# Dilated values of three head pairs made first with tokens on the partitions, and token factors spread by transposes

## The reference, cut to what matters

```
y = rms_norm(h) * g
qkv = (y @ w_qkv).reshape(B, S, 3, 3 groups, 8 heads, 64)        # 1024 x 4608 weights
for each group:  s = q k^T / 8 + bias over keys t - j*dilation;  m = max s;  p = exp(s - m)
                 den = sum p;  num = p v
o = (sum over groups of num * exp(m - m_all)) / (sum of den * exp(m - m_all))
h = h + o @ w_out
```

## Time and profile before

| | |
|---|---|
| median of 3 runs | 1863.96 us (1863.92 to 1864.14) |
| the profiled execution | 1863.83 us, span in the trace 1862.1 us |
| granted TensorE clock | 0.999 |
| TensorE busy | 1850.5 us, 99% of the span |
| TensorE weight loads busy | 1535.1 us, 82% |
| VectorE busy | 1127.5 us, 61% |
| ScalarE busy | 672.8 us, 36% |
| GpSimd busy | 165.3 us, 9% |
| chain that ended last | PE 94%, DVE 5% |

### The profile page before, as it was taken

The page is one execution under the profiler, slowest core; times in us unless marked ns, Lnnn a source line. Parts: engine busy times, 40 slices in busy tenths (PEclk is TensorE's granted clock), DMA queues, the critical chain, the costliest instruction groups (busy, mean ns, idle before and its releaser), DMA issues.

```text
span 1862.1 us, 24221 instructions
## 1 busy us (share of the span) xinstructions
PE 1850.5 (99%) x8817; PEld 1535.1 (82%) x8817; DVE 1127.5 (61%) x1524; ACT 672.8 (36%) x975; POOL 165.3 (9%) x199
## 2 busy tenths in 40 slices
PE   9999999999999999999999999999999999999998
PEld 7888888888888888888888888888888878888887
DVE  7888788676676444686642354366776786325532
ACT  6323434343333333344321222225555653212221
POOL 0011112200000011002000000101211220000000
PEclk9999999999999999999999999999999999999999
DMA  4222222323233333223333343322222123333232
GB/s 161 81 89 80 80 68 80 113 91 101 90 101 94 109 103 125 84 75 93 119 101 93 115 121 97 104 93 71 78 69 80 47 90 113 102 93 100 90 102 68
DMA packets 55156, 175.29 MB, mean 94 GB/s; under 512 B 6201, under 2 KB 12857, under 8 KB 55074
## 3 DMA queue, kind: packets, MB, share of 16 engines
q1 hardware_dynamic: 49744, 170.43, 29.4%
q10 hardware_dynamic: 4818, 3.68, 0.9%
q0 software_dynamic: 512, 0.03, 0.0%
HBM read 171.96 MB, written 2.13 MB: 93 GB/s over the span
## 4 chain that ended last, share of the span: by engine, by line
PE 94%; DVE 5%; DMA 0%; issue 0%; ACT 0%; SPq 0%; DVEq 0%; ACTq 0%
PE ps L605 30%; PE ps L607 29%; PE ps L606 29%; PE ps L1101 1%; DVE wlo L1621 1%; PE ps L1132 1%; PE ps L1113 1%; PE ps L613 1%; PE ps L903 1%; PE ps L893 0%; DVE yr L1640 0%; DVE grm L1713 0%; PE ps L1144 0%; PE ps L980 0%; DVE h L2286 0%
## 5 line engine op out<-in xcount | busy, mean ns | idle before, releaser
L605 PE MATMUL ps<-xhi,whi 128*128 128x512 f32 x1568 | 617.2, 394 | 1.4 <-DVE wlo L1621 0.6
L607 PE MATMUL ps<-xlo,whi 128*128 128x512 f32 x1568 | 610.9, 390 | 0.0
L606 PE MATMUL ps<-xhi,wlo 128*128 128x512 f32 x1568 | 610.5, 389 | 0.0
L1621 DVE TENSOR_TENSOR wlo<-raw,whi 128x1024 fp32r<-128x1024 f32 x314 | 403.8, 1287 | 210.8 <-ACT whi L1257 210.6
L1257 ACT ACTIVATE whi<-raw 128x1024 fp32r<-128x1024 f32 x314 | 331.1, 1055 | 537.6 <-PE ps L607 475.4
L605 PEld LDWEIGHTS ps<-xhi,whi 128*128 128x128 f32 x1568 | 294.4, 188 | 64.9 <-DVE wlo L1621 1.9
L607 PEld LDWEIGHTS ps<-xlo,whi 128*128 128x128 f32 x1568 | 294.3, 188 | 62.0
L606 PEld LDWEIGHTS ps<-xhi,wlo 128*128 128x128 f32 x1568 | 294.6, 188 | 59.3
L605 PE MATMUL ps<-mh,whi 128*128 128x512 f32 (+1 forms) x528 | 202.2, 383 | 0.0
L606 PE MATMUL ps<-mh,wlo 128*128 128x512 f32 (+1 forms) x528 | 202.0, 383 | 0.0
L607 PE MATMUL ps<-mh,whi 128*128 128x512 f32 (+1 forms) x528 | 202.0, 383 | 0.0
(11 more groups left out here) (346 smaller groups left out, 1962.4 us busy)
## 6 DMA issues: line engine op xcount, KB each, us to landing
raw<-wst SPq DMA_DIRECT2D x314, 512.0 KB, 3.5
h<-xT SPq DMA_DIRECT2D x8, 256.0 KB, 5.6
out<-h SPq DMA_DIRECT2D x8, 256.0 KB, 2.2
raw<-wst SPq DMA_DIRECT2D x4, 256.0 KB, 5.4
bias_a<-bias_rows ACTq DMA_DIRECT2D x4, 256.0 KB, 4.6
bias_b<-bias_rows ACTq DMA_DIRECT2D x4, 256.0 KB, 4.4
wsf<-wsT ACTq DMA_DIRECT2D x1, 512.0 KB, 3.4
bsb<-bs ACTq DMA_DIRECT2D x1, 512.0 KB, 4.3
```

Of the source, the lines that this page charges most:

```text
L605: pe.matmul(o, w[0], x[0], start=first, stop=False, **kw)
L606: pe.matmul(o, w[1], x[0], start=False, stop=False, **kw)
L607: return pe.matmul(o, w[0], x[1], start=False, stop=done, **kw)
L1621: dve.tensor_tensor(wlo[:, n % SLOTS, :], raw[:, n % 2, :], whi[:, n % SLOTS, :].bitcast(F32), ALU.subtract).then_inc(s_split, 1)
```

## The change

The 36 units of the dilated stage become 12 units `dv` and 27 units `dil`.

**`dv`: values of pairs 0 to 2 first.** For each group (f = 0 to 2 for groups 1, 2, 0 of the weights) four units hold rows of two k tiles each and 512 columns of V, of which the first 384 (pairs 0 to 2) are used. Now x is the stationary operand: 128 tokens (every fourth for f < 2) x 128 features, and 384 weight columns stream. Output: 128 tokens x 384 in each of four banks (`V_BANKS`). The norm stands behind the first of the 12 units. ScalarE reads the banks with the token's inverse rms as a scale (`v_kept_of`): pair 0 into `dvt`, pairs 1 and 2 kept in `vf` and `oM`; VectorE makes the low part of pair 0. The inverse rms with tokens on the partitions (`rtv`) comes over DRAM by three DMAs of GpSimd. GpSimd splits the kept values of pairs 1 and 2 into `dvt` between its steps (`kept_v_split`).

**`dil`: 27 units.** Pairs 0 to 2 have 6 units each (q and k), pair 3 has 9. All steps of pairs 0 to 2 come every 3 ticks. The last pair's v units are transposed as before (`v_turned`, 3 instead of 12), and both factor rows of pairs 0 to 2 go through bank 7, so that the second waits for the first's product (`s_fml`).

**Token factors** (lines 965 and 1055) are spread by `pe.transpose` where fp32 matmuls did it.

The diff, cut:

```diff
-          ("dil", 36), ("dilout", 4),
+          ("dv", 12), ("dil", 27), ("dilout", 4),
...
-DIL_UNITS = 36
+DIL_UNITS = 27
 LOGITS_AT, TURN_AT, SUMS_AT = {}, {}, {}
 V_TURN_AT, V_SPLIT_AT = {}, {}
 RESCALE_AT, WEIGHTS_AT, WIDEN_AT = {}, {}, {}
-for _p in range(4):
-    _d, _l = TICKS * (9 * _p + 6) - 1, TICKS * (9 * _p + 9)
-    for _s in range(4):
-        _n = 8 * _p + _s
-        LOGITS_AT[_d + 3 * _s], TURN_AT[_d + 3 * _s + 2], SUMS_AT[_d + 3 * _s + 5] = _n, _n, _n
-        _n += 4
-        if _p < 3:
-            _late = 1 if _s == 0 else 0
-            LOGITS_AT[_l + 5 * _s + 1 + _late], TURN_AT[_l + 5 * _s + 3 + _late] = _n, _n
-            SUMS_AT[_l + 5 * _s + (8 if _s < 3 else 7)] = _n
-        else:
-            LOGITS_AT[_l + (-2, -1, 1, 2)[_s]], TURN_AT[_l + (0, 1, 3, 4)[_s]], SUMS_AT[_l + 2 + _s] = _n, _n, _n
-    for _o in range(3):
-        _k = TICKS * (9 * _p + 3 * (_o + 1))
-        V_TURN_AT[_k + (1 if _k < TICKS * DIL_UNITS else 0)] = 3 * _p + _o
-        V_SPLIT_AT[_k + (2 if _k < TICKS * DIL_UNITS else 0)] = 3 * _p + _o
-    RESCALE_AT[_l + (18 if _p < 3 else 4)] = _p
-    WEIGHTS_AT[_l + (19 if _p < 3 else 5)] = _p
-    WIDEN_AT[_l + (20 if _p < 3 else 6)] = _p
+for _p in range(3):
+    for _s in range(8):
+        _n, _t = 8 * _p + _s, TICKS * (6 * _p + 4) + 3 + 3 * _s
+        LOGITS_AT[_t], TURN_AT[_t + 2], SUMS_AT[_t + 5] = _n, _n, _n
+    RESCALE_AT[_t + 2], WEIGHTS_AT[_t + 3], WIDEN_AT[_t + 4] = _p, _p, _p
+_l = TICKS * DIL_UNITS
+for _s in range(4):
+    _n, _t = 24 + _s, _l - 13 + 3 * _s
+    LOGITS_AT[_t], TURN_AT[_t + 2], SUMS_AT[_t + 5] = _n, _n, _n
+    _n += 4
+    LOGITS_AT[_l + (-2, -1, 1, 2)[_s]], TURN_AT[_l + (0, 1, 3, 4)[_s]], SUMS_AT[_l + 2 + _s] = _n, _n, _n
+RESCALE_AT[_l + 4], WEIGHTS_AT[_l + 5], WIDEN_AT[_l + 6] = 3, 3, 3
+for _o, _t in enumerate((_l - 23, _l - 10, _l)):
+    V_TURN_AT[_t], V_SPLIT_AT[_t + (1 if _o < 2 else 0)] = _o, _o
 PAIRED = STEPS - 4
 MULTIPLIED_AT = {}
 for _t, _n in LOGITS_AT.items():
     if _n >= PAIRED:
         MULTIPLIED_AT[_t] = (_n,)
     elif _n % 2 == 0:
-        MULTIPLIED_AT[_t - (3 if _n % 8 == 6 else 1)] = (_n, _n + 1)
+        MULTIPLIED_AT[_t - 1] = (_n, _n + 1)
 FACTOR_ROWS_AT = {}
 FACTORS_ON_AT = {}
 for _p in range(3):
     for _part in range(2):
-        FACTOR_ROWS_AT[TICKS * 9 * (_p + 1) + 22 + 3 * _part] = _p, _part
-        FACTORS_ON_AT[TICKS * 9 * (_p + 1) + 23 + 3 * _part] = _p, _part
-OUT_SPLIT_AT = {65: 0, 101: 1, 138: 2}
+        FACTOR_ROWS_AT[TICKS * 6 * _p + 46 + 2 * _part] = _p, _part
+        FACTORS_ON_AT[TICKS * 6 * _p + 47 + 2 * _part] = _p, _part
+OUT_SPLIT_AT = {53: 0, 77: 1, 102: 2}
 PART_AT = {TICKS * DIL_UNITS + _m: _m for _m in range(8)}
-OUT_HI_AT = {148: 0, 151: 1, 152: 2}
-OUT_LO_AT = {149: 0}
+OUT_HI_AT = {TICKS * DIL_UNITS + 4: 0, TICKS * DIL_UNITS + 7: 1, TICKS * DIL_UNITS + 8: 2}
+OUT_LO_AT = {TICKS * DIL_UNITS + 5: 0}
+V_BANKS = (2, 3, 4, 5), (0, 1, 6, 7), (2, 3, 4, 5)
...
         def factor_bank(p, part):
-            return bank(6) if part else bank(7 if p < 3 else 2)
+            return bank(7) if p < 3 else bank((2, 6)[part])
+        def v_tokens(f, t):
+            return slice(t, T, NT) if f < 2 else slice(t * P, (t + 1) * P)
+        def v_columns(f, t):
+            return rtv[:, (4 if f == 2 else 0) + t:(4 if f == 2 else 0) + t + 1]
+        def v_kept(p, o):
+            if o:
+                return vf[:, 1 + 2 * (o - 1):3 + 2 * (o - 1), :].rearrange("p a b -> p (a b)").rearrange(
+                    "p (t x c) -> p t x c", x=2, c=P)[:, :, p - 1, :]
+            return (oM[:, :] if p == 1 else vf[:, 0, :]).rearrange("p (t c) -> p t c", c=P)
+        def qkv_of(k):
+            return (k // 6, k % 6 // 2, k % 2) if k < 18 else (3, (k - 18) // 3, k % 3)
...
-                        ins = pe.matmul(bank(7 - n)[:, t * P:(t + 1) * P], rtk[:, NT * n + t:NT * n + t + 1].to_broadcast([P, P]), ident,
-                                        start=t == 0, stop=True, skip_group_check=True)
+                        ins = pe.transpose(bank(7 - n)[:, t * P:(t + 1) * P], rtk[:, NT * n + t:NT * n + t + 1].to_broadcast([P, P]), ident)
...
-                    ins = pe.matmul(bank(6)[:, t * P:(t + 1) * P], rtok[:, t:t + 1].to_broadcast([P, P]), ident, start=t == tiles[0],
-                                    stop=True, skip_group_check=True)
+                    ins = pe.transpose(bank(6)[:, t * P:(t + 1) * P], rtok[:, t:t + 1].to_broadcast([P, P]), ident)
...
                 if n % 4 == 0:
-                    pe.wait_ge(s_dvs, 3 * p + (3 if part else 2))
+                    if p == 0:
+                        pe.wait_ge(s_dve, 12 if part else 8)
+                    elif p < 3:
+                        pe.wait_ge(s_dvs, 3 * (p - 1) + (3 if part else 2))
+                    else:
+                        pe.wait_ge(s_dv3, 3 if part else 2)
                 if n:
                     pe.wait_ge(s_dco, n if n <= PAIRED else n - 1)
                 if n == STEPS - 1:
                     pe.wait_ge(s_dlg, STEPS)
-                if n % 8 == 0 and n:
-                    pe.wait_ge(s_fml, 2 * p)
...
             def v_turned(v):
-                pe.wait_ge(s_free, A0["dil"] + 3 * (v + 1))
+                pe.wait_ge(s_free, A0["dil"] + 18 + 3 * (v + 1))
                 if v:
-                    pe.wait_ge(s_dvs, v)
-                if v in (4, 7, 10):
-                    pe.wait_ge(s_fml, 2 * (v // 3) - 1)
+                    pe.wait_ge(s_dv3, v)
+                if v == 1:
+                    pe.wait_ge(s_fml, 6)
                 for t in range(NT):
-                    src = dvf[:, t * P:(t + 1) * P] if v % 3 == 2 else dvf[:, t::4]
+                    src = dvf[:, t * P:(t + 1) * P] if v == 2 else dvf[:, t::4]
                     ins = pe.transpose(bank(7)[:, t * P:(t + 1) * P], src, ident)
...
             def factor_rows(p, part):
                 pe.wait_ge(s_wid, 2 * p + part + 1)
-                if part or p == 3:
+                if p == 3:
                     pe.wait_ge(s_dco, 8 * p + 8)
-                else:
-                    pe.wait_ge(s_dvs, 3 * p + 4)
+                elif part:
+                    pe.wait_ge(s_fml, 2 * p + 1)
+                elif p == 2:
+                    pe.wait_ge(s_dv3, 1)
                 for t in range(NT):
...
-            for k in range(36):
-                xs = x_tile if k else fresh(x_tile, s_x, X0["down01"])
-                own = dict(banks=(DIL_BANK,) * 2, free=True) if k == 2 else {}
-                dense(U0["dil"] + k, A0["dil"] + k, full(1), xs, tick=lambda q: attend(TICKS * k + q), **own)
-                if k == 0:
-                    norm("down01")
-            for tick in range(TICKS * 36, LAST_TICK):
+            for f in range(3):
+                for j in range(4):
+                    u = U0["dv"] + 4 * f + j
+                    unit_ready(u)
+                    for k in (2 * j, 2 * j + 1):
+                        if f == 0:
+                            pe.wait_ge(s_x, X0["down01"] + k + 1)
+                        elif k == 0 and f == 1:
+                            pe.wait_ge(s_free, A0["dil"])
+                            pe.wait_ge(s_rb, N0["down01"] + 1)
+                        elif k == 0:
+                            pe.wait_ge(s_dve, 4)
+                        c0 = (k % 2) * T
+                        for t in range(NT):
+                            c = v_tokens(f, t)
+                            ins = mm3(pe, bank(V_BANKS[f][t])[:, 0:3 * P], (xhi[:, k, c], xlo[:, k, c]),
+                                      (whi[:, u % SLOTS, c0:c0 + 3 * P], wlo[:, u % SLOTS, c0:c0 + 3 * P]), k == 0, k == KD - 1)
+                    ins.then_inc(s_unit, 1)
+                    if f == 0 and j == 0:
+                        norm("down01")
+            pe.wait_ge(s_dve, 8)
+            for k in range(DIL_UNITS):
+                if k == 4:
+                    pe.wait_ge(s_dve, 12)
+                dense(U0["dil"] + k, A0["dil"] + k, full(1), x_tile, tick=lambda q: attend(TICKS * k + q))
+            for tick in range(TICKS * DIL_UNITS, LAST_TICK):
...
+            def v_kept_of(f):
+                if f != 1:
+                    act.wait_ge(s_rtw if f else s_rtv, 16)
+                act.wait_ge(s_unit, U0["dv"] + 4 * f + 4)
+                for t in range(NT):
+                    v, r = bank(V_BANKS[f][t]), v_columns(f, t)
+                    act.activation(dvt[:, f, t, 0::3, :], v[:, 0:P].rearrange("p (x d) -> p x d", d=DH), ACT.Copy, scale=r)
+                    if f == 0:
+                        act.activation(v_kept(1, 0)[:, t, :], v[:, P:2 * P], ACT.Copy, scale=r)
+                        ins = act.activation(v_kept(2, 0)[:, t, :], v[:, 2 * P:3 * P], ACT.Copy, scale=r)
+                    else:
+                        both = vf[:, 2 * f - 1 + t // 2, (t % 2) * 2 * P:(t % 2 + 1) * 2 * P]
+                        ins = act.activation(both, v[:, P:3 * P], ACT.Copy, scale=r)
+                    ins.then_inc(s_dvh, 1)
```

(81 more changed lines are left out.)

10 lines of the change are left out of this document (6 added, 4 removed).

## The result

The changed kernel takes 1873.59 us, median of five runs (1873.29 to 1873.84), against 1863.96 of the kernel before (five runs in turn with it): ratio 1.0049 with an interval of 1.0037 to 1.0060. It is 9.6 us slower, where 2.3 us faster was forecast; it lies above the range (1859.5 to 1867.0) and 1.0 above rival A's 1872.6. The spans of the two traces differ by 9.8 us.

A forecast was written before the change was run, and what follows sets the result against it. TensorE's queue was taken to set the end. The terms 0.94 - 3.8 + 1.2 - 0.9 - 0.4 + 0.7 gave -2.3 us, so 1861.7 us, 0.12% faster, with a range of 1859.5 to 1867.

The forecast's parts named there:

- rival A: First two V stages: strided weight loads are not hidden behind 384 columns, +10.9 us, giving 1872.6; chance 0.11.
- (1): V projections on TensorE: 288 matmuls of 384 columns replace 216 of 512, +0.94 us; strided loads charged nothing.
- The upper bound: V projections: a strided load takes twice about 0.115 us, 0.23, so 192 loads add +10.9 us at most.
- (2): Transposes of V on TensorE: nine of twelve groups of four go, -3.8 us.
- (3): The norm: TensorE reaches it earlier and waits for the split of the sums of squares, +1.2 us.
- (4): Token factors spread by transposes: -0.9 us in TensorE's queue and -0.4 us at the very end.
- (5): Attention steps moved to every three ticks: `v_turned(1)` waits at bank 7 for VectorE's factor product, +0.7 us.
- (6): VectorE, ScalarE and GpSimd in the denser attention: their work, GpSimd's value splits included, stays hidden; charged nothing.
- rival B: Changes of pair in the attention: VectorE's arrears stall TensorE, 1 to 2 us each, 1864.7 to 1867.7; chance 0.17.

The follow-up runs named there:

- e8: The kernel before, with each group of four transposes of a V tile issued four times over: 1881.28 us, one run.
- e1: The changed kernel with the first two V stages reading 128 tokens in a row, not every fourth: 1863.57 us, ratio 0.9995 to the kernel before.
- e9: The changed kernel with GpSimd copying x for contiguous loads, both small attention waits removed and the norm's surroundings reordered: 1859.91 us, ratio 0.9975 to the kernel before.
- e5: The changed kernel with GpSimd's split of a kept value tile one step earlier and the last pair's factors one tick earlier: 1870.91 us, ratio 1.0036.

## Why the prediction was wrong

The step that failed is in part (1): "So the stride costs some 0.01 us a load, and 0.10 a load is well under 0.173. [...] I take nothing, since the strided rows are the nearest." The load of V's stationary x at a 16-byte step takes 0.233. The rows of the transposes were near in place and stride and not in kind: the load of a transpose stays at 0.12 or less at this very stride (e8), so its 0.01 us says nothing of a load that goes from hidden to 0.233. The reading was a little off as well: 0.39 / 4 is not the distance of the strided starts, which are up to 0.12 apart in rows 5 too. The upper bound, twice the densest pace of loads, came within 0.003 us of 0.233. In part that is luck: no run measures the pace of contiguous loads that the doubling starts from. Rows 13 already held a hint: strided loads of dvf at 200 to 212 ns, contiguous ones at 137.

- (1) Pitch of 384 columns, 0.1733: right (0.1734 in the third stage, 0.173 in e1 everywhere). Stride: forecast nothing, measured 192 x 0.0594 = **+11.4**; rival A's place, mechanism and price (+10.9) were right, its chance of 0.11 was low for what spoke in its favour.
- (2) The removed transposes, -3.8: not run by themselves. e9 has none of the waits and no slow loads, and its dilated part is 3.2 us shorter than in the kernel before (247.87 against 251.05). With the 0.94 of the extra starts that leaves **-4.1** for (2) and whatever else the moved steps changed.
- (3) The norm's wait: forecast +1.2; in the changed kernel 0, because the slow loads bring TensorE there 1.4 us later; with fast loads 1.16 (e1). A right wait that another error covered.
- (4) The spreads, -0.9 and -0.4: measured -0.91 by the rows, and 0.23 (0.46 to 0.23) plus 0.27 (0.72 to 0.45) on the chain.
- (5) The wait of `v_turned(1)`: forecast 0.7; its transposes start 1.11 us behind the last dense matmul instead of 0.23, 0.88 late. Right in place, releaser and size:
```profile
1462.18 0.40 PE L629 MATMUL ps<-xlo,whi 128*128 128x512 f32 x1
1463.29 0.72 PE L1169 MATMUL ps<-con,dvf 128*128 128x128 f32 x4 [0.71 <-DVE oA L2244]
```
- (6) No stall from the denser steps: half right. Of VectorE's arrears nothing came, so rival B is out in its own mechanism. But stalls at two changes of pair are there, 0.75 us each, **+1.5**, through a door that the part left open: it gave GpSimd's splits a price on GpSimd and none on VectorE beside them (e5).

The sum with measured terms: 0.94 + 11.4 - 4.1 + 0 - 0.9 - 0.5 + 0.9 + 1.5 = +9.2 us. The spans differ by 9.8, and 0.5 of that lies in front of the change: its first changed instruction starts at 753.58 against 753.10, where other traces of the same code have 752.78 to 753.51. Within the dilated part the terms give 0.94 + 11.4 - 4.1 + 0.9 + 1.5 = 10.6, and the trace has 10.64.

## What to carry to other kernels

Before swapping which operand is stationary, look at the step in bytes at which its columns are read: here the load hid behind 384 columns at 8 bytes and almost at 12, at 16 bytes it took 0.233 us and even 512 columns did not hide it. If a strided operand is used many times, a copy in the wanted order on an idle engine, made while other work needs nothing from it, pays (e9). Price a step by rows of the same kind of instruction. Where only another kind has the stride, neither its difference nor its ratio between strided and contiguous carries over (0.120 to 0.109 here, against 0.233 to less than 0.173): give the bound more weight, or run the one line that shows it, as e1 does.
